# A two-layer diffusion block on one core: the last up projection on un-normalised activations, and partial sums moved to GpSimd

## What is computed

```
def layer_norm(x, g, b):
    mu = mean(x); var = mean((x - mu)**2)
    return (x - mu) * rsqrt(var + LN_EPS) * g + b

def modulate(h, shift, scale):  return h * (1.0 + scale) + shift
def swiglu(u, w_up, w_down):    a, v = split(u @ w_up, 2); return (silu(a) * v) @ w_down

h = post_norm(h, mods[5] * y, ln_g[l, 1], ln_b[l, 1])          # y: mixer output times w_o
h = post_norm(h, 0.5 * mods[8] * swiglu(modulate(h, mods[6], mods[7]), ffn2_up[l], ffn2_down[l]), ...)
```

## Time and profile before

| | us |
|---|---|
| median of 3 runs | 2446.35 |
| lowest and highest | 2445.7, 2447.71 |
| the profiled execution, device time | 2447.26 |
| its span | 2445.4 |
| PE busy | 2403.1 |
| DVE, ACT, POOL busy | 1527.8, 1049.7, 3.9 |
| mean granted TensorE clock | 0.993 |

### The profile page before, as it was taken

One profiled execution on the slowest core, in us unless ns is written; L12 is line 12 of the kernel. 1 busy time (PEld: TensorE's weight loads), 2 busy tenths in 40 slices (PEclk: granted clock), 3 DMA queues, 4 the chain that ended last, 5 costly groups with the idle time before them and its releaser, 6 DMA issues.

```text
span 2445.4 us, 36162 instructions
## 1 busy us (share of the span) xinstructions
PE 2403.1 (98%) x13312; PEld 2069.9 (85%) x13312; DVE 1527.8 (62%) x2551; ACT 1049.7 (43%) x2078; POOL 3.9 (0%) x8
## 2 busy tenths in 40 slices
PE   7999999999999999999999999999999999998998
PEld 4888889887888778888888898888898898998998
DVE  6777467445545455668774367786566556676655
ACT  6433324434333434364333254333254453555444
POOL 0000000000000000000000000000000000000000
PEclk9999999999999999999999999999999999998999
DMA  8566354232222322326663326664434333554654
GB/s 277 179 187 184 101 173 122 78 95 70 69 61 69 95 78 74 108 81 199 187 187 94 97 83 204 191 180 138 134 101 115 104 107 101 164 152 125 196 166 121
DMA packets 519672, 320.79 MB, mean 131 GB/s; under 512 B 14022, under 2 KB 481520, under 8 KB 519536
## 3 DMA queue, kind: packets, MB, share of 16 engines
q1 hardware_dynamic: 518088, 318.59, 44.8%
q10 hardware_dynamic: 1448, 0.38, 0.1%
HBM read 317.87 MB, written 1.05 MB: 130 GB/s over the span
## 4 chain that ended last, share of the span: by engine, by line
PE 89%; DVE 3%; ACT 3%; issue 2%; DMA 2%; SPq 1%; ACTq 0%; DVEq 0%
PE ps L889 26%; PE ps L891 26%; PE ps L890 25%; PE ps L1137 2%; PE ps L948 1%; PE ps L949 1%; PE ps L950 1%; PE ps L876 1%; PE ps L1152 1%; ACT w_hi L1288 1%; DMA raw<-in_ffn_up 1%; PE ps L1113 1%; PE ps L1171 1%; SPq L689 1%; DVE h L1915 0%
## 5 line engine op out<-in xcount | busy, mean ns | idle before, releaser
L1781 DVE TENSOR_TENSOR w_lo<-raw,w_hi 128x1024 fp32r<-128x1024 f32 (+3 forms) x432 | 489.1, 1133 | 595.7 <-ACT w_hi L1288 594.5
L889 PE MATMUL ps<-u_hi,w_hi 128*128 128x512 f32 (+1 forms) x2368 | 860.0, 363 | 1.2 <-DVE w_lo L1781 1.2
L891 PE MATMUL ps<-u_hi,w_lo 128*128 128x512 f32 (+1 forms) x2368 | 847.7, 358 | 0.0
L890 PE MATMUL ps<-u_lo,w_hi 128*128 128x512 f32 (+1 forms) x2368 | 847.0, 358 | 0.0
L1288 ACT ACTIVATE w_hi<-raw 128x1024 fp32r<-128x1024 f32 (+3 forms) x432 | 425.8, 986 | 915.0 <-PE ps L891 815.6
L891 PEld LDWEIGHTS ps<-u_hi,w_lo 128*128 128x128 f32 x2368 | 447.2, 189 | 65.9
L889 PEld LDWEIGHTS ps<-u_hi,w_hi 128*128 128x128 f32 x2368 | 447.6, 189 | 64.3 <-issue 1.7
L890 PEld LDWEIGHTS ps<-u_lo,w_hi 128*128 128x128 f32 x2368 | 447.7, 189 | 62.9
L889 PE MATMUL ps<-g_hi,w_hi 128*128 128x512 f32 (+1 forms) x704 | 243.8, 346 | 0.0
L891 PE MATMUL ps<-g_hi,w_lo 128*128 128x512 f32 (+1 forms) x704 | 241.2, 343 | 0.0
L890 PE MATMUL ps<-g_lo,w_hi 128*128 128x512 f32 (+1 forms) x704 | 241.2, 343 | 0.0
(11 more groups left out here) (276 smaller groups left out, 2959.2 us busy)
## 6 DMA issues: line engine op xcount, KB each, us to landing
raw<-in_ffn_up SPq DMA_DIRECT2D x152, 512.0 KB, 3.9
raw<-in_w_in SPq DMA_DIRECT2D x132, 512.0 KB, 3.8
ada_in_up<-in_w_ada SPq DMA_DIRECT2D x108, 512.0 KB, 4.0
raw<-in_ffn_down SPq DMA_DIRECT2D x67, 384.0 KB, 3.3
raw<-in_ffn_down SPq DMA_DIRECT2D x42, 320.0 KB, 3.2
h<-in_ffn_up SPq DMA_DIRECT2D x22, 512.0 KB, 3.9
ada_in_down<-in_w_ada SPq DMA_DIRECT2D x20, 512.0 KB, 4.2
stage<-in_w_ada SPq DMA_DIRECT2D x16, 512.0 KB, 11.3
```

The source lines that it names most:

```text
L889: pe.matmul(ps[bank][:, cols_of], wh, a_hi, start=a, stop=False)
L890: pe.matmul(ps[bank][:, cols_of], wh, a_lo, start=False, stop=False)
L891: m = pe.matmul(ps[bank][:, cols_of], wl, a_hi, start=False, stop=b)
L1781: dve.tensor_tensor(lo, whole, hi.bitcast(F32), ALU.subtract).then_inc(lo_done, 1)
```

## The change

For the last norm in front of an up projection (n = 5, `DEFERRED`), the norm is no longer applied before the matmuls. With x the pivoted h, a and b the per-channel scale and shift, m the rest of the mean and s the inverse deviation, the modulated input is (x - m) s a + b, so a product with weights w is s (w·(a x) - m (w·a)) + w·b.

- ACT writes the high part of a x straight from h (`scaled_high`), DVE the low part with one `scalar_tensor_tensor` for each tile (`scaled_low`), both among the wo tiles.
- `extra_columns` (four small DVE instructions) puts -a and b, split, into two columns behind the 256 tokens. Each matmul of the 44 up chunks takes 258 columns (`WIDE`), and gives w·(a x), -w·a and w·b.
- `statistics` and `spread` of n = 5 move from before the up projection into `interleaved`, after its steps 4 and 6.
- For each of the 44 chunks, ACT copies the two extra columns out of PSUM, DVE moves the chunk out of PSUM with m times -w·a added (128x256), and POOL multiplies it by s (128x256). Silu runs in place with w·b as its bias, and DVE adds w·b of the second chunk and multiplies. The results of a pair are finished while the next pair's first chunk is evacuated, one chunk later than before.
- Mean and scale of h itself, which the residual needs, are applied in the second body of the loop on DVE, the residual's factor in the third on ACT.
- In the wo stages of both layers the sums of tiles 4, 5 and 6 (`add_rest` and `add_squares`) move from DVE to POOL (`late_sums`), 6 instructions in layer 1 and 12 in layer 0.

```diff
+POOL_TILES = (4, 5, 6)
+DEFERRED = 5
+WIDE = SEG + 2
...
+            if n == DEFERRED:
+                pe.wait_ge(extra_ready, 1)
...
+                    own = slice(0, WIDE) if n == DEFERRED else seg
+                    pe.matmul(ps[q][:, own], wh, u_hi[:, k, own], start=(k == 0), stop=False)
...
+                if n == DEFERRED:
+                    if step == 4:
+                        statistics(n, 0)
+                    if step == 6:
+                        spread(n, 0)
...
+            def deferred(i):
+                for q in range(4):
+                    pe.wait_ge(up_moved, 4 * i + q - 3)
+                    chunk(base + q + 4 * i, (base + q) % SPLIT, q, of(u_hi, u_lo, range(KD), slice(0, WIDE)),
+                          slice(0, WIDE))
...
     ACT:
+                for q in range(4):
+                    ahead(base, q, i, 4)
+                    act.wait_ge(chunk_used, base + q + 1 + 4 * i)
+                    act.activation(up_col[:, q, :], ps[q][:, SEG:WIDE], ACT.Copy).then_inc(up_cols, 1)
+                    if q % 2:
+                        act.wait_ge(up_cols, 4 * i + q)
+                        act.wait_ge(up_scaled, 4 * i + q)
+                        act.activation(scr[q // 2][:, lat], scr[q // 2][:, lat], ACT.Silu,
+                                       bias=up_col[:, q - 1, 1:2]).then_inc(evac_act, 1)
+                    elif not (isinstance(i, int) and i == q == 0):
+                        deferred_high(2 * i + q // 2 - 1, 1 - q // 2)
+                    if isinstance(i, int) and i == 2:
+                        act.wait_ge(ln_xn, xn_count(n, 0, 2 * q + 1))
+                        residual(n, (2 * q, 2 * q + 1))
...
-            squares(n, (0, 1, 2, 3))
+            squares(n, (0, 1, 2))
+            if n == DEFERRED:
+                scaled_high(n, (0, 1, 2))
+            squares(n, (3,))
...
+                scaled_high(n, (3,))
                 squares(n, (4,), 0)
                 ahead(base, 0, 1, 4)
                 squares(n, (5,), 0)
+                scaled_high(n, (4, 5))
                 ahead(base, 1, 1, 4)
-                squares(n, (6, 7), 0)
+                squares(n, (6,), 0)
+                scaled_high(n, (6,))
+                ahead(base, 2, 1, 4)
+                squares(n, (7,), 0)
+                scaled_high(n, (7,))
+                ahead(base, 3, 1, 4)
                 deviation(n, 0)
...
     POOL:
+        def late_sums(n):
+
+            for order, (_, seg) in enumerate(seg_order(n)):
+                for k in POOL_TILES:
...
+                    pool.tensor_tensor(scr[5][:, seg], a, h[:, k, seg], ALU.add).then_inc(rest_added, 1)
+                    pool.wait_ge(ln_sq, squares_before(n) + own + 1)
+                    pool.wait_ge(ln_added, added_before(n) + own - 1)
+                    pool.tensor_tensor(scr[2][:, seg], scr[2][:, seg], scr[1][:, seg], ALU.add).then_inc(ln_added, 1)
...
+        pool.wait_ge(up_spread, 2)
+        for n in range(CH_UP):
+            own = scr[n % 4 // 2 + (2 if n % 2 else 0)][:, SEG:TOK]
+            pool.wait_ge(up_moved, n + 1)
+            pool.tensor_tensor(own, own, inverse_std, ALU.mult).then_inc(up_scaled, 1)
...
     DVE:
+                for q in range(4):
+                    ahead(base, q, i, 4)
+                    dve.wait_ge(chunk_used, base + q + 1 + 4 * i)
+                    dve.wait_ge(up_cols, 4 * i + q + 1)
+                    dve.scalar_tensor_tensor(scr[q // 2 + 2 * (q % 2)][:, lat], delta, up_col[:, q, 0:1],
+                                             ps[q][:, 0:SEG], ALU.mult, ALU.add).then_inc(up_moved, 1)
+                    if not (isinstance(i, int) and i == 0 and q < 2):
+                        (deferred_low if q % 2 else deferred_product)(2 * i + q // 2 - 1, 1 - q // 2)
...
+            def deferred_product(p, e):
+                dve.wait_ge(up_scaled, 2 * p + 2)
+                dve.wait_ge(evac_act, a0 + p + 1)
...
+            if n == DEFERRED:
+                extra_columns()
...
+                add_squares(n, (1, 2))
+                scaled_low(n, 0)
+                scaled_low(n, 1)
                 dve.wait_ge(chunk_used, base + 5)
                 late_branch(n, 4, 0, 0)
                 centre(n, (5, 6, 7))
-                add_rest(n, 4, 0)
-                add_squares(n, (1, 2, 3))
+                add_squares(n, (3,))
+                scaled_low(n, 2)
                 ahead(base, 0, 1, 4)
-                add_squares(n, (4,), 0)
                 dve.wait_ge(chunk_used, base + 6)
                 late_branch(n, 5, 1, 0)
-                add_rest(n, 5, 0)
-                add_squares(n, (5,), 0)
                 ahead(base, 1, 1, 4)
+                scaled_low(n, 3)
                 dve.wait_ge(chunk_used, base + 7)
                 late_branch(n, 6, 2, 0)
-                add_rest(n, 6, 0)
-                add_squares(n, (6,), 0)
+                ahead(base, 2, 1, 4)
                 dve.wait_ge(chunk_used, base + 8)
                 late_branch(n, 7, 3, 0)
                 add_rest(n, 7, 0)
                 add_squares(n, (7,), 0)
-                taken = without_mean(n, 0)
...
+                scaled_low(n, 4)
                 ahead(base, 3, 1, 4)
+                variance(n, 0)
+                inverse(n, 0)
```

More of the change, by code:

```diff
@@ L947, in interleaved @@
                     wh, wl = (w[:, (base + q) % SPLIT, k * P:(k + 1) * P] for w in (w_hi, w_lo))
[L948 to L950 removed]
+                    own = slice(0, WIDE) if n == DEFERRED else seg
+                    pe.matmul(ps[q][:, own], wh, u_hi[:, k, own], start=(k == 0), stop=False)
+                    pe.matmul(ps[q][:, own], wh, u_lo[:, k, own], start=False, stop=False)
+                    m = pe.matmul(ps[q][:, own], wl, u_hi[:, k, own], start=False, stop=(k == KD - 1))
                     if nth == len(items) - 1:
@@ L967, in up @@
             interleaved(base, n)
+            def deferred(i):
[4 more added lines that the diff above has]
+            if n == DEFERRED:
+                deferred(1)
+                deferred(2)
+                with pe.Fori(3, UP_BODIES) as i:
+                    deferred(i)
+                return
             def body(i):
@@ L1249, in mixer @@
                     part(e, 1, segs[0][1])
-                statistics(n, 0)
-                spread(n, 0)
         for layer in range(DEPTH):
@@ L1349, in modulate, with scaled_high @@
                     m.then_inc(u_hi_done, 1)
+        def scaled_high(n, ks):
+            for k in ks:
+                if k < pivot_tiles(n):
+                    act.wait_ge(ln_cent, KD * (n - 1) + centre_index(n, k) + 1)
+                else:
+                    act.wait_ge(evac_dve, branch_done(n, k, 0))
+                if k == 0:
+                    act.wait_ge(cols_mod, n + 1)
+                m = act.activation(u_hi[:, k, 0:SEG], h[:, k, SEG:TOK], ACT.Identity, scale=mod_a[:, k, 1:2],
+                                   bias=small[:, 1:2])
+                if k == ITEM[ITEM_OF[k]][-1]:
+                    m.then_inc(u_hi_done, 1)
         def residual(n, ks):
@@ L1396, in up, with deferred, deferred_high @@
             n = 3 * layer + 2 * f
+            lat = slice(SEG, TOK)
+            def deferred(i):
+                for q in range(4):
[12 more added lines that the diff above has]
+                        residual(n, (2 * q, 2 * q + 1))
+            def deferred_high(p, e):
+                act.wait_ge(evac_dve, d0 + 1 + p)
+                act.activation(g_hi[:, p, lat], scr[2 + e][:, lat], ACT.Copy).then_inc(g_hi_done, 1)
+            if n == DEFERRED:
+                for i in range(3):
+                    deferred(i)
+                with act.Fori(3, UP_BODIES - 1) as i:
+                    deferred(i)
+                deferred(UP_BODIES - 1)
+                deferred_high(KF - 1, 1)
+                return
             def body(i):
@@ L1709, in mixer @@
                 squares(n, (5,), 0)
+                scaled_high(n, (4, 5))
                 ahead(base, 1, 1, 4)
-                squares(n, (6, 7), 0)
+                squares(n, (6,), 0)
[4 more added lines that the diff above has]
+                ahead(base, 3, 1, 4)
                 deviation(n, 0)
-                ahead(base, 2, 1, 4)
-                modulate(n, 0, (0, 1))
-                ahead(base, 3, 1, 4)
-                modulate(n, 0, range(2, KD))
+                act.wait_ge(ln_mean, segs_before(n) + 1)
+                act.activation(delta, mean_of[0][:, SEG:TOK], ACT.Copy).then_inc(up_spread, 1)
+                act.wait_ge(ln_spread, segs_before(n) + 1)
+                act.activation(inverse_std, spread_of[0][:, SEG:TOK], ACT.Copy).then_inc(up_spread, 1)
             silu_table()
@@ L2066, in body, with deferred, deferred_low @@
                     ada_add(block - begin + i, (block - begin + (i if isinstance(i, int) else PEELED)) // ADA_BLOCKS)
+            n, lat, taken = 3 * layer + 2 * f, slice(SEG, TOK), []
+            def deferred(i):
+                for q in range(4):
```

(29 more changed lines are left out.)

58 lines of the change are left out of this document (30 added, 28 removed).

## The result

| | before | after |
|---|---|---|
| median | 2446.02 us | 2455.68 us |
| lowest and highest of 6 | 2444.19, 2447.71 | 2454.42, 2456.55 |
| span of the profiled execution | 2445.4 | 2454.0 |

The ratio is 1.0038, with a 95% interval of 1.0027 to 1.0049: the changed kernel is slower by 9.7 us. The time lies inside the range, near rival 1's 2457.

The account below looks back on a forecast made before the run. PE, busy 2403.1 of 2445.4 us, was taken as the bound, so only its stops or half clock could give much. Start -5.4, clock +3.6, columns +0.8, loop +2.1, late sums -1.2 gave -0.1: 2446.2 us, range 2439 to 2459.

Parts of the forecast that it names:

- rival 1: Loop of up1: POOL's SBUF reads and DVE's two-input instructions exclude each other; pair 6.1 to 6.3 us, 2457 us; chance 0.32.
- The start: Start of up1: norm leaves the path, mostly replaced by waits for weight splits; chunk 4 earlier, -5.4 us.
- The clock: Start of up1: two stops of 2.2 and 2.5 us make PE's clock fall to half, +3.6 us.
- The bound of 4.0: Clock fall's price, at most 4.0 us: first 96 matmuls of up1 took 15.6 us against 11.6.
- The extra columns: Up1's 960 matmuls behind the first 96: two more columns cost 0.0008 us each, +0.8 us.
- The loop of up1: Chain of a pair fits under PE's 5.8 us; only waits in two bodies cost, +2.1 us (0 to 4).
- two bodies: Second and third loop bodies carry extra DVE and ACT work; PE waits 0.6, 1.2 and 0.3, +2.1 us.
- a chain of 5.3 us: Loop of up1: recurring chain over ACT and DVE per pair, 5.3 us, 0.5 us to spare against PE.
- the late product: End of up1's loop: last product but one comes one chunk later; costed at nothing, 1 us at worst.
- Behind the loop: From the down projection's first matmul on; the prediction's sum had no term for it.
- Late sums in layer 0: Layer 0's wo stage: twelve sums moved off DVE shorten the 2.17 us wait, -1.2 us (0 to -2.2).

Follow-up runs that it names:

- e1: Changed kernel with the 44 multiplications by the inverse deviation on DVE instead of POOL; 2452.09 us, ratio 1.0015 to 1.0034.
- e7: Changed kernel with the edits of e5 and e6, the second and third body's work spread, and ACT splitting up chunks ahead of late tiles' squares; 2439.39 us.
- e9: The combined kernel e7 with the 44 multiplications on DVE instead of POOL; 2437.2 us, ratio 0.9949 to 0.9974.
- e2: Changed kernel with each POOL multiplication replaced by a write of zeros to an unused area, scaling left out; 2444.38 us, ratio 0.9981 to 0.9999.
- e5: Changed kernel with one edit on ACT: a finished pair's high part stands behind the next weight split instead of ahead of it; 2441.44 us.
- e8: Changed kernel with POOL multiplying by the constant 1.0 (one SBUF input) instead of the inverse deviation, scaling left out; 2449.51 us, one run.
- e10: The combined kernel e7 with extra_columns behind tile 3's branch, and silu table and first loop split ahead of the inverse deviation's copy; 2435.39 us.
- e3: Kernel before the change, with only layer 0's twelve late sums moved from DVE to POOL; 2444.7 us, ratio 0.9986 to 1.0004.
- e6: Changed kernel where the last down projection's first matmuls wait for bank 0's move, not the last pair but one's product; 2455.48 us.
- e11: The combined kernel e7 with the late sums of both layers back on DVE, POOL only multiplying; 2438.8 us, ratio 0.9954 to 0.9980.

## Why the prediction was wrong

**The start: right, in size and in cause.** Forecast -5.4 for chunk 4's start with a full clock, the trace has it 6.35 earlier, of which about 1 us comes from ahead of the pivot. The waits forecast for splits were 2.2, 2.5, 1.0 and 1.0; the trace has 2.51, 0.91, 0.77 and 1.05, and e1, which keeps the full clock, 2.52, 2.27, 0.77 and 1.05. `extra_columns` cost 0.5 (1.63 against 1.16), forecast 0.6.

**The clock: wrong by 3.6.** It fell, for 3.4 us only, against 13.7 in the earlier trace rows. Windows of after (length, PE, granted clock, DMA):

```profile
2227.00:2228.00 1.00, 1.00 (x6) 0.50 0.10 22
2230.00:2231.00 1.00, 0.15 (x1) 0.82 0.02 5
```

And it cost nothing: e1, with the granted clock at 1.00 throughout the start, needs 33.99 us from the pivot to chunk 4, after 33.97. In e1 the second wait for a split is 2.27 us instead of 0.91. The slower matmuls filled a wait for DVE. Where the fall comes later, behind the last wait for a split, it has a price: 1.5 us between e7 and e9, which have the same lists there (32.2 against 30.6). Behind the second wait (e2, e5 and e8) it costs 0.5, 34.5 against 34.0. I had taken 3.6 from a stretch in which PE was the late engine and the clock low for four times as long. The bound of 4.0 was too wide as well, for 1.0 of it was a stop that I had passed over:

```profile
2239.26 0.58 PE L948 MATMUL ps<-u_hi,w_hi 128*128 128x256 f32 x1 [1.02 <-DVE u_lo L1905]
```

**The extra columns: right in some kernels, and so by luck.** 258 columns take 0.1208 us (mean over 2295 to 2345 in e5 and e7), 256 took 0.1200: 960 x 0.0008 = 0.8. But in e9 and e10 258 columns took 0.1200 as well, and cost nothing (last section). A price by the column, as I had summed it, isn't what the runs show.

**The loop of up1: the step that failed.** The forecast let POOL and DVE run side by side, with "none of it" on PE's path, and had +2.1 for two bodies and a chain of 5.3 us that "fits with 0.5 us to spare". Both parts failed. POOL's reads stretched a DVE split by 0.53 us in each pair: with POOL only writing (e2) the stretch is 119.3 us, +3.7 on before, near the forecast's +2.9 (2.1 + 0.8), and with its reads 128.8. So 9.5 of the 10.3 us that the loop's forecast lacked go with them. Measured in after: +13.2 - 0.8 = 12.4, in listed waits 2.5, pairs of 6.05 instead of 5.80 for 14.5 pairs 3.6, the stop 5.6, and some 0.7 in waits too short to be listed. (The two bodies' 2.5 against my 2.1 is luck: in e5, with the same work in them, they are gone.)

The chain I summed was not the one that closes. I followed ACT's two splits; the closed loop goes over one split on ACT and both on DVE (high part, split on ACT, split, move, low part, split, move, product), and is 5.51 without contention (e2). That leaves 0.29 us to spare and not 0.5, less than the 0.53 of the contention. The step behind it failed as well: I said the late product costs "nothing, 1 us at worst". It costs what DVE is behind at that point, and with no room in the loop that is the full lead of PE.

For a POOL instruction I had taken 0.65 us; it took 0.74 alone and 0.85 to 0.92 beside DVE. Rival 1 had the mechanism, 6.1 to 6.3 for a pair against 6.05, and the stop of 5 us; that its 2457 is so near is in part luck, as it lies midway between a sum with 3.6 us for the clock and one without, has 1 us for the wo stages, where none shows, and nothing for the 1.8 us behind the loop.

What held it at one in three was the remark that no row showed such a pair; the rows couldn't, since before has POOL idle but for its memsets. That nothing in the trace showed the two at work together was not quite so. One memset of POOL (423.70) ran beside a split that took its usual 1.22 us. A memset only writes, so that this doesn't speak against rival 1:

```profile
423.35 1.22 DVE L1781 TENSOR_TENSOR w_lo<-raw,w_hi 128x1024 fp32r<-128x1024 f32 x1
```

The Trainium skill states the rule, "SBUF — State Buffer", section Who interferes with whom, with the addition that a GpSimd instruction which only writes doesn't contend. By that page both e2 (1.22 us beside a memset of 0.74) and after (1.76 beside a multiplication) come out as measured. It calls the shared ports an exclusive lock; that the first to start keeps it for its whole instruction it spells out for another kind of DVE instruction, and for this one that was my reading. It fits after, where POOL's remaining 0.67 us (2298.20 to 2298.87) cost 0.53, and doesn't fit e8, where 0.78 us cost 0.19.

**Behind the loop: missed.** +1.8 us. Behind the stop of 5.6 us the clock fell again, from 2370.3 to 2377.1; e2, with a stop of 0.76 and no fall there, has 79.0 against after's 80.7:

```profile
2371.00:2373.00 2.00, 0.00 (x0) 0.50 0.70 195
```

**Late sums in layer 0: right.** Forecast -1.2, measured -1.5 from the pivot of layer 0 to the first up matmul: its wait is 0.67 instead of 2.17 us. That it starts 1.9 us earlier has 0.4 from ahead of the stage. By whole times (e3) nothing can be told.

```profile
1060.19 0.38 PE L962 MATMUL ps<-u_hi,w_hi 128*128 128x256 f32 x1 [0.67 <-DVE u_lo L2007]
```

So the forecast summed to -0.1 and the trace to +8.6: loop 10.3 more and its end 1.8 more, clock 3.6 less.

## What to carry to other kernels

Before moving work to another engine, find the loop that closes over the engines in a steady state: start at a wait in one engine's list, and follow what stands behind it in the same list, back to what it waits for. In these runs work and contention inside that loop cost their full length once it exceeded PE's period (6.05 and 5.85 against 5.80), and below it they still decided how fast DVE regained what it was behind. Here one move in ACT's list (a long wait put behind the next weight split instead of ahead of it) was worth 14 us, and behind it no whole time tells on which engine the added work was done.

The stop at the start of the next stage was the sum of what DVE had fallen behind before: taking away the wait that showed it (e6) moved the stop and left the time.

## What the runs showed of the hardware

- A DVE instruction on two SBUF inputs that began 0.18 us into a POOL multiplication of 128x256 took 1.76 us instead of 1.23. The other way round, POOL's sum of 128x256 that began 0.16 us into a DVE split took 1.65 us against 0.74 alone (after, layer 0). In both directions the later one lost the rest of the earlier one, less about 0.15 us: 0.53 us longer for a rest of 0.67 (after), 0.49 for 0.64 and 0.40 for 0.56 (e5, splits of 2286.15 and 2298.46), 0.91 for 1.05 (the POOL sum). The one-input multiplication of e8 is the exception.

```profile
1050.50 1.65 POOL L1842 TENSOR_TENSOR scr<-h 128x256 f32<-128x256 f32 x1 [4.36 <-DVE h L2065]
1052.11 0.74 POOL L1845 TENSOR_TENSOR scr<-scr,scr 128x256 f32<-128x256 f32 x1
```

- A multiplication by a constant on POOL (one input) is slower than one of two inputs, 0.96 to 1.02 us against 0.85 to 0.92, both beside DVE.
- Half clock for 3 us was free where PE waited for another engine anyway (33.97 against 33.99 us), 0.5 behind the second of three such waits (e2, e5, e8), and 1.5 us where no such wait was left (32.2 against 30.6).
- In e9 and e10, 258 columns took 0.1200 us, as 256 do, and in e2, e5, e7, e8 and e11 0.1208, though e7 and e10 have the same loop; after and e1 have both paces in their loops. The cause wasn't looked for.
